# The first quarter of the input loaded through ScalarE's queue instead of SyncE's, in a two-block transformer kernel

## The reference

```python
def rmsnorm(x, g):
    y = x * rsqrt(mean(x * x, axis=-1) + EPS) * g
def first_block(x, ...):
    h = rmsnorm(x, g_pre)
    proj = h @ w_in                      # 1024 x 3792
    (qa, ka, va, gate_a, qi, ki, wi, qb, kb, vb, fb, gate_b) = split(proj)
    ...                                  # sparse attention, forgetting attention, merge, gated output
def second_block(x, mem, ...):
    for i in range(2):                   # pooling / block attention, memory attention, 4096-wide MLP
        ...
```

## Time and profile before

| | us |
|---|---|
| device time, median of 3 runs | 810.45 (809.80 to 810.87) |
| device time of the profiled execution | 810.04 |
| span of the profiled execution | 808.2 |
| TensorE busy | 797.9, 99% of the span |
| VectorE, ScalarE, GpSimd busy | 537.1, 416.1, 110.3 |
| first product of unit 0 (TensorE, L1776) starts | 6.53 |
| first product of unit 2 (TensorE, L1744) starts | 18.85 |

### The profile page before, as it was taken

The page is one execution under the profiler, slowest core; times in us unless marked ns, Lnnn a source line. Parts: engine busy times, 40 slices in busy tenths (PEclk is TensorE's granted clock), DMA queues, the critical chain, the costliest instruction groups (busy, mean ns, idle before and its releaser), DMA issues.

```text
span 808.2 us, 11167 instructions
## 1 busy us (share of the span) xinstructions
PE 797.9 (99%) x4190; PEld 662.9 (82%) x4190; DVE 537.1 (66%) x728; ACT 416.1 (51%) x589; POOL 110.3 (14%) x143
## 2 busy tenths in 40 slices
PE   8999999999999999999999999999999999999998
PEld 6998977778878777888888888887777888888886
DVE  5647988767585767566665566578875666665561
ACT  5646656554655554365444435448654545444440
POOL 1610300000020510030000000067920000000000
PEclk9999999999999999999999999999999999999999
DMA  8961444345736633646655556461324466655541
GB/s 312 322 197 41 157 157 157 117 160 215 253 135 233 212 120 105 208 141 201 218 174 202 185 182 204 157 208 53 118 91 157 157 213 222 204 191 202 168 149 53
DMA packets 76742, 140.43 MB, mean 174 GB/s; under 512 B 2936, under 2 KB 23104, under 8 KB 76704
## 3 DMA queue, kind: packets, MB, share of 16 engines
q1 hardware_dynamic: 74608, 134.03, 49.3%
q0 software_dynamic: 1936, 5.82, 2.2%
q10 hardware_dynamic: 160, 0.07, 0.0%
HBM read 138.86 MB, written 1.05 MB: 173 GB/s over the span
## 4 chain that ended last, share of the span: by engine, by line
PE 89%; DVE 5%; ACT 2%; DMA 2%; issue 1%; SPq 0%; POOL 0%; DVEq 0%; ACTq 0%
PE bank L1744 57%; PE bank L2123 13%; PE bank L2125 7%; PE bank L1910 2%; PE bank L2127 2%; DVE w_lo L1184 2%; PE bank L1825 2%; PE bank L1971 1%; PE bank L1878 1%; PE bank L1945 1%; DMA raw<-in_w_in 1%; DVE prob L1356 1%; PE bank L1758 1%; DMA raw<-in_w_mem_kv 1%; PE bank L1951 0%
## 5 line engine op out<-in xcount | busy, mean ns | idle before, releaser
L1744 PE MATMUL bank<-w_hi,a_both 128*128 128x512 f32 (+2 forms) x752 | 234.5, 383 | 0.5 <-PE bank L1744 0.4
L1184 DVE TENSOR_TENSOR w_lo<-raw,w_hi 128x2048 fp32r<-128x2048 f32 (+2 forms) x65 | 146.2, 2250 | 51.8 <-ACT w_hi L727 51.4
L1627 DVE TENSOR_TENSOR w_lo<-raw,w_hi 128x2048 fp32r<-128x2048 f32 x48 | 110.0, 2292 | 91.5 <-ACT w_hi L1087 90.5
L2123 PE MATMUL bank<-a_both,w_hi 128*128 128x512 f32 x448 | 161.4, 399 | 0.0
L1744 PEld LDWEIGHTS bank<-w_hi,a_both 128*128 128x128 f32 x752 | 140.7, 188 | 22.9 <-issue 1.9
L1087 ACT ACTIVATE w_hi<-raw 128x2048 fp32r<-128x2048 f32 x48 | 92.0, 1917 | 111.9 <-PE bank L1744 53.4
L1744 PE MATMUL bank<-w_hi,b_hi 128*128 128x512 f32 x376 | 148.9, 396 | 0.1
L727 ACT ACTIVATE w_hi<-raw 128x2048 fp32r<-128x2048 f32 (+1 forms) x63 | 119.1, 1893 | 56.4 <-PE bank L1744 34.3
L1744 PE MATMUL bank<-w_lo,b_hi 128*128 128x512 f32 x376 | 146.5, 390 | 0.0
L1744 PE MATMUL bank<-w_hi,b_lo 128*128 128x512 f32 x376 | 146.5, 390 | 0.0
L1744 PE MATMUL bank<-w_lo,a_both 128*128 128x512 f32 (+2 forms) x376 | 141.7, 377 | 0.0
(11 more groups left out here) (244 smaller groups left out, 855.3 us busy)
## 6 DMA issues: line engine op xcount, KB each, us to landing
raw<-in_w_ff SPq DMA_DIRECT2D x64, 1024.0 KB, 5.2
raw<-in_w_in_moba SPq DMA_DIRECT2D x20, 512.0 KB, 4.2
raw<-in_w_merge SPq DMA_DIRECT2D x8, 1024.0 KB, 5.1
raw<-in_w_out SPq DMA_DIRECT2D x8, 1024.0 KB, 5.1
m<-in_w_in SPq DMA_DIRECT2D x6, 880.0 KB, 8.8
raw<-in_w_mem_kv SPq DMA_DIRECT2D x4, 1024.0 KB, 5.2
raw<-in_w_ple_gate SPq DMA_DIRECT2D x4, 1024.0 KB, 5.0
raw<-in_w_in_pool SPq DMA_DIRECT2D x4, 1024.0 KB, 5.1
```

What stands on the lines that cost most here:

```text
L1184: dve.tensor_tensor(w_lo[:, v % RING, 0:n], landing[land_slot(v)][:, 0:n], w_hi[:, v % RING, 0:n].bitcast(F32), ALU.subtract).then_inc(lo_ ...
L1627: dve.tensor_tensor(w_lo[:, (base + c) % RING, :], raw[:, (base + c) % RAW, :], w_hi[:, (base + c) % RING, :].bitcast(F32), ALU.subtract). ...
L1744: ins = pe.matmul(banks[t][:, 0:n], xa[:, kt, ts], wa[:, slot, w], start=first and k == 0 and q == 0, stop=last and k == kts - 1 and q == 2)
L2123: pe.matmul(b_hid[f][:, :].rearrange("p (q n) -> p q n", q=2), w_hi[:, slot, w], both_, start=kt == 0, stop=False)
```

## The change

The load of quarter 0 of `x` is no longer the first issue of SyncE. It is the first issue of ScalarE, ahead of `ident` and `pre_rows`, with the same semaphore. The issues that follow it on SyncE keep their order.

```diff
@@ SyncE
-            load_x(0, 1, x_landed)
             load_half(0, 0, half_landed)
             load_x(1, 1, x_second_landed)
             load_half(0, 2, raw_landed[0])
@@ ScalarE
+            act.dma_start(x[:, :, 0:2 * P], a["x"][0].rearrange("(t p) n -> p t n", p=P)[:, :, 0:2 * P])\
+               .then_inc(x_landed, 16)
             act.dma_start(ident[:], a["c_ident"]).then_inc(early_landed, 16)
             act.dma_start(pre_rows, a["g_pre"][0].rearrange("(k p) -> k p", p=P)).then_inc(pre_landed, 16)
             act.sem_inc(free_a, 2)
```

## The result

The changed kernel takes 813.24 us (median of 6 runs, 812.68 to 813.64) against 809.95 for the kernel before, run beside it: ratio 1.0040, 95% interval 1.0029 to 1.0051. It is 3.3 us slower, beyond the 0.2% that counts here, and outside the forecast range. The profiled execution took 812.97 us, its span is 811.2, 3.0 above. From here the lines of the changed kernel are one higher than before in the TensorE and VectorE parts (the transposes are L1826, the first products L1777).

What follows compares the result with a forecast made beforehand. TensorE, 99% busy, was taken to bound the kernel, its opening a race of weights and gains. Gains 1.03 us later, less 0.1 and 0.14, gave +0.8 on the 810.45 median: 811.2 us, range 809.9 to 812.4.

Steps and rivals of the forecast that it cites:

- SyncE's side: SyncE's loads, each issued about 0.50 us sooner: gain taken as 0, with 0.2 us kept for the range.
- the conversion from L to the end: TensorE's opening: first product at L + 1.56, 1.03 us later, less 0.1 and 0.14, so the end +0.8 us.
- L: Landing time of `g_pre` on ScalarE's queue: near 4.55 us before, 6.0 after the change, bounds 5.8 and 6.6.
- The constant: Part of a load's landing time besides packet time, calibrated on three earlier landings: 3.35 us, from 3.20 to 3.49.
- the first sharing: Quarter 0 on ScalarE's queue alternating one to one with half unit 0 on SyncE's: 1.86 us, upper bound 2.21.
- The second sharing: The identity on ScalarE's queue alternating one to one with quarter 1 on SyncE's: 0.71 us, upper bound 0.91.
- the third rival: SyncE's queue gets two packets for one of ScalarE's: `g_pre` lands at 7.5, time 812.75 us; chance 0.13.
- the later issue "alone": `g_pre` delayed only by ScalarE's extra issue: landing at 5.05 us, the lower bound, with no cost at the end.
- the first rival: Queues alternate in runs of some 16 pieces, sparing the identity quarter 1: `g_pre` lands at 5.5, 810.75 us; chance 0.27.

Runs made afterwards that it cites:

- e2: The changed kernel with six warm-up products on TensorE in place of three: 811.87 us, ratio 1.0026.
- e4: The kernel before with the identity loaded in two parts on ScalarE, one issue more: 812.22 us, ratio 1.0031.
- e9: The changed kernel with quarter 0 behind identity and `g_pre` on ScalarE, and SyncE's second load 512 KB of `x` in place of 256 KB: 815.91 us.
- e12: The kernel before with the identity in two loads on ScalarE and half of `g_pre` (2 KB) as SyncE's first load: 810.34 us, ratio 1.0008.
- e1: The changed kernel with quarter 0 moved behind the identity and `g_pre` on ScalarE: 814.79 us, ratio 1.0062.
- e8: The kernel before with `g_pre` first on SyncE, quarter 0 second on ScalarE behind the identity, and four warm-ups in place of three: 810.58 us.
- e7: The kernel before with the identity in two loads on ScalarE and five warm-ups in place of three: 810.88 us, ratio 1.0012.
- e5: The changed kernel with quarter 1 of `x` ahead of the first weights on SyncE: 813.22 us, ratio 1.0034.
- e3: The kernel before with one warm-up product in place of three: 810.46 us, ratio 1.0010.

## Why the prediction was wrong

**What held.** The weights did not come sooner for being issued sooner, since the DMA engines were full: SyncE's side was priced at 0, and the copy of unit 1's first half came 0.06 us sooner. The later gains are on the path that was named: the identity and `g_pre` behind quarter 0. And the conversion from L to the end was right. With the measured L of 6.8 to 7.0 it gives 1.03 + (0.8 to 1.0) - 0.24 = 1.6 to 1.8 us; e2, in which L is late and the pace is not lost, has unit 2 at 20.64, 1.79 late, and 2.1 us more by the runs. L before, taken as 4.55, was right as well: the trace has 4.47.

**First step that failed: the sharing between the identity and quarter 1.** L was put at 5.8 to 6.6, with 6.0 taken; it was 6.99 for the identity in the changed kernel, and 6.6 for the identity and 6.77 for `g_pre` in e2, which has the same loads. The sum had three terms. The constant and the first sharing, quarter 0 with half unit 0 at one packet to one, gave 5.2 for quarter 0, and it landed at 5.4: from 2.6 to 4.6 us the queues moved 232 packets and 231. The second sharing, the identity with quarter 1, was priced at 0.71 us, also at one to one, with 0.91 as its bound. It measured 6.99 - 5.43 = 1.56 in the changed kernel and 1.2 in e2. From 4.8 to 6.4 us the queues moved 304 packets to 163, nearly two to one. The prediction took its ratio from 2.4 to 3.0 us and laid the 78 to 34 of the earlier trace rows to a queue running dry; from 2.2 to 3.6 us, about the whole of the identity's stretch in the kernel before, it was 280 to 149. So the third rival was wrong for the first stretch and near the measurement for the second, where its 288 packets beside the identity's 144 are 1.5 us. Why the one stretch was shared evenly and the other not was not tried.

The turns of e4, e9 and e12 are a thing that the working left out too, but they do not explain the identity here: it was second on its queue, and half unit 0 was nearly through when its own queue let it start, at 4.7 us. For `g_pre`, now third and by turns behind quarter 1, they may add the 0.16 us by which it followed the identity in e2. They do show that the later issue "alone", which the prediction put at 5.05 and at no cost, costs more than its half microsecond: in e4 it gave 5.49, and 0.31%. The rule of the Trainium skill, DMA: Bandwidth & Descriptors, "Queues, rings and completion order", which gave the first rival its 810.75, would have L at 5.5; the landing at 6.99 decides against that sum. The rule speaks of bursts within an engine, and the waiting by whole loads in e9 and e12 is something else.

**Second step, and the larger miss: a term that was absent.** TensorE's warm-ups end at 4.66; with the gains later than that TensorE pauses, and every instruction up to 10.9 us ran at the lower clock: 0.46 us more for the transposes, 0.46 for the warm-up, 0.77 for the first products, a part of it hidden. It costs 1.2 to 1.4 us (e2). The prediction counted the pause as time only. It even quoted the warm-ups' row, and did not ask what they were there for. The clock row of all nines was read as full speed throughout, which the durations of the warm-ups contradict.

With both, 1.8 + (1.2 to 1.4) = 3.0 to 3.2 us, against 3.34 in the profile and 3.3 in the runs.

## What to carry to other kernels

Ahead of the first product, order loads by who needs them first, and count whole loads on both queues: a small load that everything waits for belongs to the first turn, opposite a load that is needed as early, and one more load ahead of it, on its own queue, can cost the wait for a load of the other queue. Take a ratio of sharing from the whole stretch in which a load moves and not from a window inside it. Where warm-ups cover the wait for a landing, a load that slips past their end costs the pause and then slow products. Read instruction durations for the clock at the start: the row shows full clock ahead of the record's first entry, whatever the clock was. Moving a load to another queue leaves its bytes on the same engines, so price it by what now stands ahead of whom.

## What the runs showed that was not expected

- ScalarE's loads start in turns with SyncE's. ScalarE's third load began at 4.9 us when SyncE's first two were 0.71 MB and at 5.8 when they were 0.97 MB (e1, e9). Its second began at 3.2 behind quarter 0; behind 2 KB it landed 0.7 us sooner after its issue (e4, e12). What in the hardware does it, and whether SyncE's loads wait for ScalarE's in the same way, was not tried.
- The identity had about one packet moved for two of SyncE's queue, before and after the change, while quarter 0 on the same queue had one for one. Why is open.
- The first weight packets after the start took about 0.22 us each in e8, 69 ns later. Why is open; with `x` in front it did not occur.
- TensorE at the lower level takes 1.80 us for four products of 440 columns, at the higher 1.04; a granted clock of 0.50 stood in the rows only in e9, though the warm-ups ran at the lower level in every profile. The rise came at 4.8 us in the kernel before and at 7.9 in e7, with TensorE unbroken at work from 1.73 in both; after a pause it came at 11.0 in the changed kernel, at 12.7 in e5, at 9.3 in e4 and at 8.6 in e3.
